# New opening, turned h outside the ring, and two ring slots filled earlier, in a one-core transformer layer kernel

## The chip, the cores and the metric

The kernel runs on one core of one Trainium2 chip. The metric is the device time of one execution in microseconds (us); lower is better. The kernel before takes 429.64 us, the median of three runs (429.25 to 429.87).

## What is computed

One layer for T = 256 tokens of width D = 1024, all in fp32:

```
xn   = rms_norm(h, norm1_g);  proj = xn @ w_in
y    = sigmoid gates * (nsa attention, pooled mixer, short convolution), each projected to D
h    = h + merged @ w_o
h    = h + hier_moe(rms_norm(h, norm2_g), router_group_w, router_expert_w, w1, w3, w2)
out  = rms_norm(h, final_norm_g)
```

`hier_moe` picks one of 4 groups per token and the best 2 of its 8 experts; `out += combine * ((silu(x@w1) * (x@w3)) @ w2)` over 32 experts with a hidden width of 256. The expert weights are 96 MB, read once.

## The kernel before

**Memory.** A ring of 22 slots of 1 MB in SBUF (128 partitions x 2048 floats) first holds the weights of the front half and many work tiles, then the expert weights. The 96 expert chunks (12 for each block of four experts: eight of w1 and w3, four of w2) go through these 22 slots. Slot 20 (SLOT_O) holds `oT`, the attention output, and later `g2b`, the second norm's weights. Slot 21 (SLOT_XHI) holds `xhi`, then `mhi`, then `h2T`, which is h turned for the router. SP issues all large transfers in one fixed order written out by hand (L453 to L564): the two tiles of x, the identity, the front chunks (each two halves, alternating over two sets of slots, a new half waiting for the last product that reads the old one), expert chunks into slots as they come free (`early`, L479), then the other 74 expert chunks, each behind a wait on `expert_used`, the count of chunks that TensorE is done with (L546 to L558).

**Opening (L644 to L662, L847 to L861, L1240 to L1292).** ACT sums the squares of both tiles of x, POOL takes the power -0.5 for both at once, DVE lays the result on two diagonals, and TensorE multiplies h by them (L1244, fp32), which turns and scales in one. ACT rounds a weight half to fp32r (`have_high`, L434), DVE takes the rest (`have_low`, L441); the same is done to the turned x (L660, L858). A product is three fp32r matmuls. The products for q need all of the first half of the q weights split before the first of them. The order is a outside, k inside.

**Middle.** Projections, attention, mixers and merge gates fill TensorE up to W_o (L1517 to L1519). For W_o there are two chunks, each of two halves.

**From W_o to the experts (L1095 to L1176, L1540 to L1610).** DVE adds W_o's result to h in four pieces, ACT sums their squares (L789), TensorE turns h with 16 transposes (L1543), ACT and DVE copy the result to `h2T`. The router product (L1552) has h2T stationary and 40 columns of router weights moving, 16 matmuls. DVE scales and biases the logits (L1116) and picks groups and experts in a row of small steps up to `mask_done`; meanwhile TensorE does six matmuls without use (`keep_busy(6)`, L1558). POOL multiplies tile 1 of h by g2b (L613), DVE makes tile 0 of xn2 (L1110), ACT scales tile 1 (L798). Slot 21 is filled when the logits are done, slot 20 when xn2 is done. TensorE then gathers the tokens of the first four experts (L1589; k = 0 to 5 ahead of the loop, 6 and 7 in it), ACT copies the first half of the gather (L812, first instruction in its loop), and the expert products begin (L1619).

**Expert loop.** Eight blocks. Each has the first products over eight chunks, silu, a transpose, four second products (L1646), each with a copy on ACT (L819), a combining product (L1656) and adds on DVE (L1202). In the fourth and eighth block, two idle matmuls follow each of the chunks q = 4 to 7.

**End (L821 to L831, L1223 to L1232, L628 to L635, L559 to L563).** ACT sums squares of h in three column ranges; POOL adds epsilon, multiplies half of tile 1 by the final weights and adds a partial sum; DVE multiplies the other half; POOL takes the power; ACT scales tile 1, DVE tile 0; SP issues four output transfers.

```
for c in range(SLOTS, NC):
    sp.wait_ge(expert_used, earlier(c) + 1)
    sp.dma_start(ring[:, AT[c]], experts[c // NQ, c % NQ]).then_inc(expert_in[AT[c]], 16)
```

## Time and profile before

| | |
|---|---|
| median of the runs | 429.64 us |
| the profiled execution's own time | 429.46 us |
| its span | 427.7 us |
| PE busy | 395.8 us (93%) |
| DVE, ACT, POOL busy | 202.1, 152.7, 14.7 us |
| DMA over the span | 140.18 MB, mean 328 GB/s |

The span runs from the first to the last instruction in the profile; 1.76 us of the execution's own time lie around it. In the page of the profile, the span is cut into 40 slices of 10.7 us. The rate of the DMA stands between 419 and 423 GB/s in nearly all slices from the 22nd to 38th, and is uneven before. PE is at 90% or more of nearly every slice up to the 20th, which says only that some matmul was in flight.

### The profile page before, as it was taken

The numbers are of one execution on the slowest core, as the hardware profiler recorded it, in microseconds if no ns is written. First come the engines' busy times: TensorE is split into PE (matmuls) and PEld (weight loads), VectorE is DVE, ScalarE is ACT, GpSimd is POOL, SyncE is SP. The second block draws the span as 40 slices with busy tenths as digits, with TensorE's granted clock in tenths as the row PEclk, the third lists the DMA queues.
The fourth block names the chain that finished last, engine by engine and source line by source line (L and its number), as shares of the span: only waits on it lengthen the run. The fifth ranks groups of instructions, "written<-read, shape, count | busy, mean of one in ns | idle before, by whom it ended". The sixth has DMA issues, their size and how long they took to land.

```text
span 427.7 us, 7303 instructions
## 1 busy us (share of the span) xinstructions
PE 395.8 (93%) x2858; PEld 269.9 (63%) x2858; DVE 202.1 (47%) x404; ACT 152.7 (36%) x260; POOL 14.7 (3%) x35
## 2 busy tenths in 40 slices
PE   1999999999999999999999999999999889698892
PEld 1999899767777777878784646454646245143361
DVE  0937493999898685683471232231131303114014
ACT  4823531738565635342312223230132213013014
POOL 2000000300000000000220000000000000000002
PEclk9999999999999999999989999999999969889897
DMA  8988999742442594557997999999999999999972
GB/s 302 399 326 335 364 387 382 296 147 98 149 156 62 185 359 161 208 198 308 424 410 313 421 419 420 421 421 418 421 421 423 421 421 422 421 421 422 421 306 98
DMA packets 21192, 140.18 MB, mean 328 GB/s; under 512 B 2608, under 2 KB 3120, under 8 KB 5040
## 3 DMA queue, kind: packets, MB, share of 16 engines
q1 hardware_dynamic: 20160, 138.32, 81.4%
q10 hardware_dynamic: 1008, 1.52, 1.0%
q8 instruction: 17, 0.28, 0.3%
q14 instruction: 7, 0.06, 0.0%
HBM read 138.78 MB, written 1.05 MB: 327 GB/s over the span
## 4 chain that ended last, share of the span: by engine, by line
issue 46%; PE 45%; DVE 5%; POOL 1%; DMA 1%; ACT 0%; POOLq 0%; ACTq 0%; DVEq 0%; SPq 0%
PE bank L1396 5%; PE bank L1397 4%; PE bank L1398 4%; PE bank L1255 4%; PE bank L1256 4%; PE bank L1257 4%; PE bank L1517 2%; PE bank L1519 2%; PE bank L1518 2%; PE bank L1358 1%; PE bank L1244 1%; PE bank L1384 1%; PE bank L1370 1%; DMA h<-in_x 1%; PE bank L1552 1%
## 5 line engine op out<-in xcount | busy, mean ns | idle before, releaser
L1619 PE MATMUL bank<-ring,kv 128*32 128x512 f32 x512 | 67.0, 641 | 12.5 <-DMA ring<-in_experts 11.9
L441 DVE TENSOR_TENSOR part<-ring,part 128x2048 fp32r<-128x2048 f32 (+1 forms) x28 | 61.9, 2219 | 21.7 <-ACT part L434 21.7
L434 ACT CAST part<-ring 128x2048 fp32r<-128x2048 f32 (+1 forms) x28 | 51.8, 1850 | 35.8 <-DMA ring<-in_front 35.7
L1202 DVE TENSOR_TENSOR h<-h,bank 128x256 f32<-128x256 f32 x64 | 27.0, 421 | 67.2 <-PE bank L1656 66.8
L1589 PEld LDWEIGHTS bank<-qcur,att 128*128 128x128 f32 x280 | 34.8, 195 | 17.4 <-issue 17.2
L1619 PEld LDWEIGHTS bank<-ring,kv 128*32 128x32 f32 x512 | 13.7, 112 | 48.0 <-issue 25.3
L1589 PE MATMUL bank<-qcur,att 128*128 128x128 f32 x280 | 39.9, 288 | 0.6 <-DVE qcur L1165 0.6
L1396 PE MATMUL bank<-part,xhi 128*128 128x512 f32 x96 | 39.3, 409 | 0.0
L1397 PE MATMUL bank<-part,xhi 128*128 128x512 f32 x96 | 37.6, 391 | 0.0
L1398 PE MATMUL bank<-part,xlo 128*128 128x512 f32 x96 | 37.6, 391 | 0.0
L1656 PE MATMUL bank<-gab,vbd 128*128 128x256 f32 x128 | 36.2, 405 | 0.7
L1255 PE MATMUL bank<-xhi,part 128*128 128x256 f32 x128 | 36.7, 287 | 0.0
L1256 PE MATMUL bank<-xlo,part 128*128 128x256 f32 x128 | 36.2, 283 | 0.0
L1257 PE MATMUL bank<-xhi,part 128*128 128x256 f32 x128 | 36.2, 283 | 0.0
L1646 PE MATMUL bank<-ring,hidT 128*32 128x256 f32 x512 | 34.3, 385 | 0.1
L814 ACT ACTIVATE cw<-bank 128x256 f32<-128x256 f32 x8 | 3.1, 383 | 85.0 <-PE bank L1619 85.0
L1656 PEld LDWEIGHTS bank<-gab,vbd 128*128 128x128 f32 x128 | 21.0, 188 | 16.1 <-DVE h L1202 10.5
L819 ACT COPY gab<-bank 128x256 f32<-128x256 f32 x32 | 11.9, 372 | 53.9 <-PE bank L1646 53.9
L1196 DVE TENSOR_TENSOR vbd<-cw,bank 128x256 f32<-128x256 f32 x8 | 3.4, 421 | 56.5 <-ACT cw L814 56.5
L1255 PEld LDWEIGHTS bank<-xhi,part 128*128 128x128 f32 x128 | 24.5, 191 | 0.8 <-issue 0.8
L1256 PEld LDWEIGHTS bank<-xlo,part 128*128 128x128 f32 x128 | 24.5, 192 | 0.0
L1257 PEld LDWEIGHTS bank<-xhi,part 128*128 128x128 f32 x128 | 24.5, 192 | 0.0
(229 smaller groups left out, 551.2 us busy)
## 6 DMA issues: line engine op xcount, KB each, us to landing
ring<-in_experts SPq DMA_DIRECT2D x96, 1024.0 KB, 17.9
ring<-in_front SPq DMA_DIRECT2D x30, 1024.0 KB, 5.4
ring<-in_projs SPq DMA_DIRECT2D x4, 512.0 KB, 4.7
ring<-in_front SPq DMA_DIRECT2D x2, 560.0 KB, 6.4
h<-in_x SPq DMA_DIRECT2D x2, 512.0 KB, 3.9
out_y<-att SPq DMA_DIRECT2D x4, 256.0 KB, 2.4
con<-in_consts SPq DMA_DIRECT2D x1, 764.0 KB, 11.0
oT<-in_vecs ACTq DMA_DIRECT2D x1, 512.0 KB, 6.4
```

Source lines behind the costliest of these rows:

```text
L434: nc.scalar.copy(high(n, half)[:, 0:c].bitcast(F32R), raw(n, half)[:, 0:c]).then_inc(hi_done, 1)
L441: nc.vector.tensor_tensor(low(n, half)[:, 0:c].bitcast(F32R), raw(n, half)[:, 0:c], high(n, half)[:, 0:c], ALU.subtract).then_inc(split_do ...
L1255: mm(dst, whi, ahi, start=start, stop=False)
L1256: mm(dst, whi, alo, start=False, stop=False)
L1257: return mm(dst, wlo, ahi, start=False, stop=stop)
L1396: mm(bank[t][:], XH[:, kk, cols], whi[:, k], start=(kk == 0), stop=False)
L1397: mm(bank[t][:], XH[:, kk, cols], wlo[:, k], start=False, stop=False)
L1398: ins = mm(bank[t][:], XL[:, kk, cols], whi[:, k], start=False, stop=(kk == KT - 1))
L1589: ins = mm(bank[2 + k // 4][:, (k % 4) * P:(k % 4 + 1) * P], xn2[:, t, k * P:(k + 1) * P], flat(sel[:, t]), start=(t == 0), stop=(t == NT ...
L1619: ins = mm(bank[0][CAP * e:CAP * (e + 1)], xgT[:, q, CAP * e:CAP * (e + 1)], expert(j, q, e), start=(q == 0), stop=(q == NQ1 - 1))
L1646: ins = mm(second_out(qt, slice(CAP * e, CAP * (e + 1))), hT[:, ht, CAP * e:CAP * (e + 1)], second_weights(j, qt, ht, e), start=(ht == 0), ...
L1656: mm(combined(t), cmbT[:, t * P:(t + 1) * P], yN[:, qt * QC:(qt + 1) * QC], start=True, stop=True).then_inc(comb_done, 1)
```

## The change

Six parts, by their place in the program:

1. Opening: the q weights' first transfers are cut in two (`first_in`); x is scaled by DVE (`scale_x`, four pieces of 512 columns), with the power taken per tile; TensorE turns it with transposes instead of products with a diagonal; four idle matmuls stand ahead; splits and products of q go by pairs of k, k outside and a inside; four small transfers of ACT's queue are issued later.
2. `h2T` moves from slot 21 to `kv` and `gab`; `g2b` moves from slot 20 to `con`. Slot 20 is filled after `oT_done`, between the two chunks of W_o in SP's order; slot 21 directly behind slots 16 to 18, at W_o's end.
3. Router: the router weights, padded to 64 columns, are stationary and h2T moves, even k in the first and odd k in the last 64 output rows; ACT copies the result, two matmuls with `fold2` add the halves and turn them back. POOL multiplies all four pieces of h by g2b, ACT scales both tiles.
4. Gather: k = 0 to 3 ahead of the loop, 4 to 7 in two pieces in it; ACT's first copy stands ahead of its loop.
5. The idle matmuls behind chunk q = 7 go.
6. End: ACT's first squares stand ahead of the last block's last copy; POOL multiplies three quarters of tile 1 early, DVE one quarter; the partial sums are one DVE instruction; the last output transfer is issued by ACT.

```diff
-            front_chunk(CH_Q, 0)
-            front_chunk(CH_Q, 1)
+            for half in range(2):
+                for sem_in, c in ((first_in[half], slice(0, 1024)), (chunk_in[slot(CH_Q, half)], slice(1024, 2048))):
+                    sp.dma_start(raw(CH_Q, half)[:, c], front[CH_Q, half, :, c]).then_inc(sem_in, 16)
...
-            for i in range(2):
-                front_chunk(CH_WO + i, 0)
-                front_chunk(CH_WO + i, 1)
+            front_chunk(CH_WO, 0)
+            front_chunk(CH_WO, 1)
+            sp.wait_ge(oT_done, 2)
+            early(SLOT_O, SLOT_XHI)
+            front_chunk(CH_WO + 1, 0)
+            front_chunk(CH_WO + 1, 1)
...
             early(SET_B + 2, SLOT_MERGED)
-            sp.wait_ge(logit_full, 1)
             early(SLOT_XHI, SLOTS)
-            sp.wait_ge(xn2_done, NT)
-            early(SLOT_O, SLOT_XHI)
...
+            for t in range(NT):
+                pool.wait_ge(ssq_done, t + 1)
+                step(nc.gpsimd.tensor_scalar(stat[:, 20 + t:21 + t], stat[:, t:t + 1], EPS, None, ALU.add))
+                nc.gpsimd.tensor_tensor(stat[:, 22 + t:23 + t], stat[:, 20 + t:21 + t], stat[:, 32:33], ALU.pow).then_inc(rstd_done, 1)
...
+            q_high(0, 0)
+            q_high(0, 1)
+            act.wait_ge(prm_in, 16)
+            x_high(0)
...
+            gathered_copy(0)
             act.wait_ge(passes_done, 1)
...
+            scale_x(0, 0)
+            scale_x(0, 1)
+            q_low(0, 0)
+            scale_x(1, 0)
+            scale_x(1, 1)
+            x_low(0)
+            x_low(1)
+            q_low(0, 1)
...
+            pe.wait_ge(zeros_set, 9)
+            keep_busy(4, pcw[:, 0, 0:P], pcw[:, 0, 0:2 * P])
+            for t in range(NT):
+                for k in range(KT):
+                    if k % 4 == 0:
+                        pe.wait_ge(scaled, 2 * t + k // 4 + 1)
+                    ins = nc.tensor.transpose(xT(k)[:, t * P:(t + 1) * P], xs[:, t, k * P:(k + 1) * P], ident)
...
-                for t in range(NT):
-                    ins = mm(bank[(0, 3)[t]][:, 0:RC], h2T[:, k, t * P:(t + 1) * P], rw[:, k], start=(k == 0), stop=(k == KT - 1))
+                ins = mm(bank[0][HD * (k % 2):HD * (k % 2) + HD, 0:T], rw[:, k], h2T[k], start=(k < 2), stop=(k >= KT - 2))
+            ins.then_inc(lgT_full, 1)
+
+            pe.wait_ge(lgT_done, 1)
+            for t in range(NT):
+                ins = mm(bank[3][:, t * RC:(t + 1) * RC], lgT[:, t * P:(t + 1) * P], fold2, start=True, stop=True)
...
-            gather(0, 1, 2, 3, 4, 5)
+            gather(0, 1, 2, 3)
...
-                        if q == 2:
-                            gather(6, 7)
+                        if q in (1, 2):
+                            gather(2 * q + 2, 2 * q + 3)
...
-                        if j == ROUND - 1 and q >= 4:
+                        if j == ROUND - 1 and 4 <= q < NQ1 - 1:
...
-                    gather(3, 4, 5)
+                    gather(3)
...
-            nc.vector.tensor_tensor(fin[:, 1, HALF:D], h[:, 1, HALF:D], fing[:, HALF:D], ALU.mult).then_inc(gained, 1)
+            nc.vector.tensor_tensor(fin[:, 1, 3 * QC:D], h[:, 1, 3 * QC:D], fing[:, 3 * QC:D], ALU.mult).then_inc(gained, 1)
+            dve.wait_ge(ssq_done, 3 * NT + 2 * NT)
+            nc.vector.scalar_tensor_tensor(stat[:, 28:30], stat[:, 12:14], EPS, stat[:, 14:16], ALU.add, ALU.add).then_inc(means_done, 1)
...
+            act.wait_ge(act_fin, 2)
+            act.dma_start(out[P:2 * P, HALF:D], fin[:, 1, HALF:D]).then_inc(out_done, 16)
```

## Rows read from the trace of the kernel before

**Rows 1.** Stages: window, its length, busy time (instructions) of each engine, clock, DMA share, GB/s.

```profile
226.80:229.60 2.80, 2.70 (x23) 1.28 (x24) 0.00 (x0) 1.13 (x1) 0.00 (x0) 1.00 0.33 56
229.60:414.40 184.80, 172.17 (x1409) 85.45 (x1412) 42.99 (x115) 39.26 (x67) 0.00 (x0) 0.95 1.01 420
```

**Rows 2.** Timeline of SP's queue around the start of the experts: start, length, what.

```profile
217.14 0.81 SPq L482 DMA_DIRECT2D ring<-in_experts  x2
...
228.02 1.19 SPq L548 DMA_DIRECT2D ring<-in_experts  x2
```

**Rows 3.** Timeline of TensorE in the last expert block (idle time and releaser in brackets).

```profile
398.24 1.94 PE L1619 MATMUL bank<-ring,kv 128*32 128x512 f32 x8 [1.42 <-DMA ring<-in_experts]
...
405.92 1.07 PE L1619 MATMUL bank<-ring,kv 128*32 128x512 f32 x8
...
416.27 1.07 PE L1646 MATMUL bank<-ring,hidT 128*32 128x256 f32 x16
```

**Rows 4.** Timeline of the opening, all engines, and SP's issue at the first q end.

```profile
4.12 1.06 ACT L649 ACTIVATE squares<-h 128x1024 f32<-128x1024 f32 x1 [1.32 <-DMA h<-in_x]
...
5.65 1.06 ACT L649 ACTIVATE squares<-h 128x1024 f32<-128x1024 f32 x1 [0.38 <-DMA h<-in_x]
...
7.28 0.71 POOL L588 TENSOR_TENSOR stat<-stat 128x2 f32<-128x2 f32 x1
...
8.56 5.61 PE L1244 MATMUL bank<-gab,h 128*128 128x128 f32 x32 [8.56 <-DVE gab L850]
9.17 1.90 ACT L434 CAST part<-ring 128x2048 fp32r<-128x2048 f32 x1 [2.37 <-DMA ring<-in_front]
11.10 2.29 DVE L441 TENSOR_TENSOR part<-ring,part 128x2048 fp32r<-128x2048 f32 x1 [2.52 <-ACT part L434]
13.31 3.22 DVE L858 SCALAR_TENSOR_TENSOR xlo<-bank,prm,xhi 128x256 fp32r<-128x256 f32 x8
...
20.11 0.33 SPq L471 DMA_DIRECT2D ring<-in_front  x1
```

**Rows 5.** Timeline of ACT and DVE at the third half of W_o's weights.

```profile
186.59 1.92 ACT L434 CAST part<-ring 128x2048 fp32r<-128x2048 f32 x1 [0.72 <-DMA ring<-in_front]
...
190.49 2.28 DVE L441 TENSOR_TENSOR part<-ring,part 128x2048 fp32r<-128x2048 f32 x1
```

**Rows 6.** Timeline from W_o's end to the first expert product; the sixth row is a window.

```profile
209.17 1.30 POOL L613 TENSOR_TENSOR att<-h,oT 128x512 f32<-128x512 f32 x1 [123.52 <-DVE h L1099]
...
213.37 3.74 PE L1552 MATMUL bank<-rw,h2T 128*128 128x40 f32 x32 [0.48 <-ACT h2T L794]
...
216.94 4.52 PE L1558 MATMUL bank<-con 128*128 128x256 f32 x12
217.15 0.43 DVE L1116 SCALAR_TENSOR_TENSOR qT<-bank,stat,rb 128x40 f32<-128x40 f32 x2 [1.26 <-PE bank L1552]
...
223.19 2.92 PE L1589 MATMUL bank<-qcur,att 128*128 128x128 f32 x24 [0.56 <-DVE qcur L1165]
...
218.00:220.00 2.00, 2.00 (x6) 1.55 (x6) 1.76 (x8) 0.22 (x1) 0.00 (x0) 0.50 0.99 401
...
224.75 1.28 ACT L812 ACT_TABLE_LOAD   x1 [3.71 <-DVE npass L1160]
...
226.90 1.93 PE L1619 MATMUL bank<-ring,kv 128*32 128x512 f32 x16 [0.57 <-ACT kv L812]
```

**Rows 7.** Chain that ended last, in order of time: products on four column strips.

```profile
43.53 1.86 PE bank L1316 x32
```

**Rows 8.** Timeline of the end: DVE, POOL, ACT and SP.

```profile
420.11 1.14 DVE L1225 TENSOR_TENSOR att<-h,con 128x512 f32<-128x512 f32 x1
...
420.65 0.65 POOL L633 TENSOR_TENSOR stat<-stat 128x2 f32<-128x2 f32 x1
...
422.38 1.33 ACT L831 ACTIVATE att<-att,stat 128x512 f32<-128x512 f32 x2 [1.77 <-POOL stat L635]
...
423.17 1.81 SPq L563 DMA_DIRECT2D out_y<-att  x4
```

More of the change, by code:

```diff
@@ L266, in build @@
         vec_in = sem("vec_in")
+        first_in = [sem(f"first_in{half}") for half in range(2)]
         chunk_in = {s: sem(f"chunk_in{s}") for s in (0, 1, 2, 3, *range(SET_A, SET_B + 4, 2))}
@@ L417, in before, with splits, q_pair @@
             return [m for m in range(n) if slot(m, 0) == slot(n, 0)]
+        def splits(n, half):
+            return 4 * (half + 1) if n == CH_Q else 8 + 2 * (SPLITS.index(n) - 1) + half + 1
+        def q_pair(half, pair):
+            return [w[:, 512 * pair:512 * (pair + 1)] for w in (raw(CH_Q, half), high(CH_Q, half), low(CH_Q, half))]
         def floats(n):
@@ L650, in _, with q_high, x_high @@
                                      scale=D ** -0.5, accum_out=stat[:, t:t + 1]).then_inc(ssq_done, 1)
+            def q_high(half, pair):
+                if pair < 2:
+                    act.wait_ge(first_in[half], 16)
+                else:
+                    landed(act, CH_Q, half)
+                r, hi, lo = q_pair(half, pair)
+                nc.scalar.copy(hi.bitcast(F32R), r).then_inc(hi_done, 1)
+            def x_high(k):
+                act.wait_ge(xT_full, k + 1 if k < 6 else KT)
+                nc.scalar.activation(xhi[:, k].bitcast(F32R), xT(k), ACT.Copy,
+                                     scale=prm[:, PR_G1 + k:PR_G1 + k + 1]).then_inc(xhi_done, 1)
+            q_high(0, 0)
+            q_high(0, 1)
+            act.wait_ge(prm_in, 16)
+            x_high(0)
+            x_high(1)
+            x_high(2)
+            q_high(0, 2)
+            x_high(3)
+            x_high(4)
+            q_high(0, 3)
+            x_high(5)
+            x_high(6)
+            x_high(7)
+            for pair in range(4):
+                q_high(1, pair)
+            have_high(act, CH_KV, 0)
             act.dma_start(flat(cw2[:]), small).then_inc(small_in, 16)
@@ L805, in _, with gathered_copy, hidden @@
             nc.scalar.activation(e2, behind, ACT.Exp).then_inc(exp_done, 1)
+            def gathered_copy(b):
+                act.wait_ge(xg_full, b * 2 + 2)
+                nc.scalar.copy(flat(xgT[:, 0:4]), bank[2][:]).then_inc(xg0_done, 1)
+            def hidden(after):
+                act.wait_ge(hid1_full, after)
+                nc.scalar.activation(sl1, bank[0][:, 0:HID], ACT.Silu).then_inc(silu_done, 1)
+                act.wait_ge(hT_full, after)
+                nc.scalar.copy(flat(hT), bank[1][:, 0:HT * P]).then_inc(hT_done, 1)
@@ L1263, in split @@
             def split(n, half):
-                pe.wait_ge(split_done, 2 * SPLITS.index(n) + half + 1)
+                pe.wait_ge(split_done, splits(n, half))
             XH, XL = xhi[:].bitcast(F32R), xlo[:].bitcast(F32R)
@@ L1280, in pair @@
                 ins.then_inc(full, 1)
-            split(CH_Q, 0)
-            w = parts(CH_Q, 0, 2 * P)
-            for a in range(2):
+            for half in range(2):
+                w = parts(CH_Q, half, 2 * P)
                 for k in range(KT):
-                    if a == 0:
+                    if half == 0:
                         pe.wait_ge(xnT_done, k + 1)
-                    ins = product(bank[4][:, a * T:(a + 1) * T], w[0][:, k, a * P:(a + 1) * P], w[1][:, k, a * P:(a + 1) * P],
-                                  XH[:, k], XL[:, k], k == 0, k == KT - 1)
-            ins.then_inc(q_full, 1)
-            pair(bank[5], CH_Q, 1, q_full)
+                    if k % 2 == 0:
+                        pe.wait_ge(split_done, 4 * half + k // 2 + 1)
+                    for a in range(2):
+                        ins = product(bank[4 + half][:, a * T:(a + 1) * T], w[0][:, k, a * P:(a + 1) * P], w[1][:, k, a * P:(a + 1) * P],
+                                      XH[:, k], XL[:, k], k == 0 and a == 0, k == KT - 1 and a == 1)
+                ins.then_inc(q_full, 1)
             pair(bank[0], CH_KV, 0, kvc_full)
```

198 lines of the change are left out of this document (111 added, 87 removed).

## The prediction

> **What bounds the kernel now.** I first cut the span at the places where the DMA's rate changes (busy time by windows). From 229.6 to 414.4 us the DMA is full: share 1.01, 420 GB/s [rows 1]. These 184.8 us carry the 74 expert chunks that do not fit in the 22 slots at first, so 184.8 / 74 = 2.50 us a chunk. In the 2.8 us before, the share is 0.33: the ring is full and nothing may be sent. SP's queue shows the ends of this gap: the last two slots are asked for at 217.14, the next chunk only at 228.02, when TensorE is done with the first one [rows 2]. TensorE's first expert product starts at 226.90 [rows 6].
>
> The reader is to see three stages. Up to 226.9 TensorE and what feeds it set the pace. From there 74 x 2.50 us follow, whatever TensorE does. Then comes a tail: in the last block TensorE waits 1.42 us for chunk q = 4 at 398.24; counting on in steps of 2.50, q = 7 arrives at 405.7 and the last of w2 at 415.7; TensorE takes q = 7 at 405.92 and the last at 416.27 [rows 3], 0.2 and 0.6 us behind.
>
> So the time is (start of the experts) + (stream) + (tail). A slot that is filled earlier shortens the stream only if the ring would not be full otherwise. It is full 2.8 us before the stream starts again.
>
> **The slots, part 2.** Two transfers of 2.50 us leave the stretch behind W_o: one goes ahead of it, one moves from the logits to W_o's end. The ring is then full about 2.5 us earlier (224.3 by the old clock, since only one transfer leaves the full stretch). Alone I book 0. It is cover for the other parts: they can pull the first freed slot from 228.0 toward 224.3 before filling would bind, 3.7 us against the 2.2 found below. The transfer into slot 20 now stands ahead of W_o's second chunk on SP's queue, its wait on `oT_done` before the waits of W_o's second chunk. 2.5 us there delay W_o's third half by 0.6 at most, since SP asks for that half only when a later product ends. ACT takes this half at 186.59 after 0.72 us of waiting, but DVE only at 190.49, 2.0 us after ACT is done [rows 5]. Cost 0; bound 0 to 0.6.
>
> **The opening, part 1.** Before: the second sum of squares runs 5.65 to 6.8, the power ends at 7.99, TensorE turns x from 8.56 for 5.6 us, and the first product waits for that and for DVE [rows 4]. The first q half ends at 20.11, where SP's next request is released; TensorE's pairs are 5.76 us apart from there. After, from the same rows:
> - Tile 0: squares end 5.3, power 1.2 later, 6.5; DVE scales two pieces. A 512-column piece costs 0.45 to 0.69 (2.29 us for 2048 columns with two inputs, a quarter is 0.6 to 0.7). Done near 7.4.
> - q weights: the full half lands at 9.17 [rows 4]; its first part, if sent first, 1.3 us before, near 7.9. ACT rounds it (a third of 1.90, 0.6), DVE splits it to 9.15, scales tile 1 to 10.1.
> - Turning follows the scaling. At 0.23 a matmul, as in the gather (2.76 / 12 [rows 6]), the last is done by 11.0; ACT, in its order, wants it only at 13.2.
> - ACT then makes eight x pieces and two quarters by 14.4, DVE eight pieces of 0.40 (3.22 / 8) and three quarters of 0.7 by 15.8 [rows 4]. The last k can start at 15.8, its six matmuls take 0.7: 16.5 to 17.2.
> - 20.1 minus 17.2 gives 2.9. The second half needs DVE's quarters at 16.5 to 18.5, TensorE wants them from 17.2 in steps of 1.4: covered.
> I take 2.6, for a part of the landing that isn't split so cleanly. Bounds: 3.2 (landing not last) and -1.5, below. The later small transfers are needed at the pooled mixer near 71 us: 0. Later front chunks are requested by TensorE's own progress, so they move along; the 2.6 reach W_o's end whole.
>
> One resource is shared here. DVE's last product takes 1.14 us while POOL is in a 1.30 us product; other tensor products of 512 columns take 0.69 [rows 8]. In the opening POOL's steps for tile 1 meet DVE's scaling of tile 0, at most 0.45 us, and tile 1 waits for the split of q until 9.15 anyway: 0 in my sum. The Trainium skill (SBUF — State Buffer, "Who interferes with whom") says that DVE and GpSimd share a port pair as an exclusive lock. By that rule POOL would stand still for two whole pieces of 0.69, tile 1's power would come at 8.0 + 1.4 = 9.4 instead, and the sum below would be 6.05. The trace agrees so far as DVE's product was drawn out beside POOL's; who gives way, it does not show.
>
> **The router, parts 2 and 3.** TensorE's 16 router matmuls run from 213.37 for 3.74 us, and DVE reads the logits at 217.15 [rows 6]. After: eight matmuls of 256 columns. On four column strips, 16 matmuls of 256 columns take 1.86 us [rows 7], 0.12 each; on two strips I take 0.24 each, 1.9 in all (bounds 1.0 and 3.8, without any overlap). ACT's copies come 0.3 earlier by the new order, so 212.95 + 1.9 = 214.9; a 256-column copy 0.4 to 0.5; two fold matmuls 0.5 (0.234 each, from 3.74 / 16). Logits at 216.0: gain 1.15, bounds -0.7 and 2.0. POOL's four products of 1.30 [rows 6] end at 213.1 as its two do now, each following h's pieces 1.35 apart; the power is ready at 214.5, ahead of need. ACT's scalings (2 x 1.15) end near 217.7, and its exponentials are wanted at 220: 0. The six idle matmuls take 4.52 us, partly at clock 0.50 [rows 6], beside DVE's choice of experts, which is as long; all at half clock (12 records of 256 columns, 0.43 each) they take 5.1 and make TensorE late by up to 0.9. I take 0.15 off.
>
> **The gather, part 4.** The 24 records are twelve matmuls and take 2.76 net (2.92 less what the last one overlaps); eight matmuls instead of twelve end 0.9 earlier. But ACT's copy now waits for a table load of 1.28 us from 224.75 [rows 6], which ends at 226.03. Ahead of the loop, a copy behind exponentials needs no load, as in the attention. The copy then starts 0.1 after the gather's end, and the product follows: 225.85 instead of 226.90. Gain 1.05 (bounds 0.4, if TensorE's loop entry is then late, and 1.3). Parts 3 and 4 together: 2.05; one more piece of the gather between the first two chunks delays the second freed slot by 1.1, hidden by 2.50 for the first.
>
> **Parts 5 and 6.** Without the idle matmuls behind q = 7 the last block is 0.7 us faster, and the shorter gather gives 1.1; only 0.6 count, since then the last chunk's arrival binds [rows 3]. The partial sum on POOL (420.65, 0.65) behind its long product, and DVE's 1.14 product, go from the path; DVE's final sum comes at 420.3 less that 0.6 instead of 421.4: 0.6. The four output requests take 1.81 [rows 8], the last now goes out on ACT beside them: 0.45. Sum 1.65, bounds 0.8 and 2.1.
>
> **Sum.** 2.6 + 2.05 + 1.65 = 6.3 us. The profiled execution took 429.46 (span 427.7), 0.18 under the median: 429.46 - 6.3 = 423.2.
>
> **Rivals.**
> - *The opening gives little* (0.17): the two parts of a weight half land together at 9.17, so DVE scales tile 1 1.2 us later, and TensorE is at its slow clock in the products. For it: the 16 turning matmuls took 0.35 each, against 0.23 for such matmuls later [rows 4, 6]. Opening about 0.5: 425.3. The Trainium skill (TensorE: Matmul & The Clock Gate, "Part 1: The HAM clock gate") says that the clock starts at half and activity releases it. By that rule the four idle matmuls at the start speak for the forecast, and the gap behind them for this rival.
> - *The front swallows the shift* (0.10): a weight chunk lands by bytes and not by request, and 2.6 us are lost before W_o: 425.8. Against: ACT and DVE have 2 us of slack at the row I checked [rows 5].
> - *The slots pay for themselves* (0.03): if the stream, not the first freed slot, were the limit, two chunks or 5.0 us more: 418.2. Against: the gap of 2.8 us.
> - *Slower* (0.05): TensorE stays at 1.2 GHz through the gappy opening and again behind the router, which is now short bursts around a copy. At half speed from 10.9 to 21 us the q products end at 27.3 instead of 25.9, a loss of 1.5; idle matmuls overrun by 0.9, and eight gather matmuls cost 1.9 more, with 0.5 for rank and count. 429.46 + 1.5 + 3.3 - 2.05 - 1.65 = 430.6. It decides if the granted clock behind 214 is 0.50 up to the gather; before it was 0.50 from 218 to 220 alone [rows 6].
> - The rest, 0.05, lies near no change.
>
> **Numbers.** The forecast has 0.60. A difference under 0.2%, 0.9 us, can hardly be told from none. Faster 0.88, same 0.05, slower 0.07. The range goes from the best bounds of all three terms, 429.46 - (3.2 + 3.3 + 2.1) = 420.9, to past both weak cases: 420.9 to 426.4.
>
> **What would show it.** SP's second request of the front for the q slot at 17.5 instead of 20.11; the first logits' row on DVE 3.6 to 3.8 earlier; no table load ahead of the first gathered copy; the first freed slot near 223.4, a longer gap in the DMA before it, and then 184.8 us at 420 GB/s again; the last w2 product within 0.1 us of its chunk; three output requests on SP. It would be wrong if the stretch at 420 GB/s got shorter by chunks, or if the first q half ended later than 19.

## The result and the profile after

The changed kernel takes 427.34 us, the median of 12 runs (426.09 to 429.89), against 429.70 us (428.79 to 430.78) for the kernel before beside it. The ratio is 0.9946, 95% interval 0.9925 to 0.9967. It is faster, by 2.3 us; the forecast was 6.3, and 427.34 lies above the range's end of 426.4.

The profiled execution of the changed kernel took 429.35 us. It belongs to an upper group of four of the 12 runs, at 429.15 to 429.89; the other eight lie at 427.5 or below. So the table below also has the profile of a repeat of the same kernel (427.12 us, near the median; 427.66 us as median of 10, ratio 0.996, interval 0.9933 to 0.9987). Each cell is a gain in us over the profile of before, between two marks in the timelines. The spans are 427.7 before, 425.3 and 427.5 after.

| step, from mark to mark | forecast | repeat | profiled |
|---|---|---|---|
| opening: SP's request at the end of the first q half (20.11; 18.85; 19.74) | 2.60 | 1.26 | 0.37 |
| from there to the logits on DVE (217.15; 214.68; 215.65) | 1.15 | 1.21 | 1.13 |
| logits to the first expert product (226.90; 223.32; 225.66) | 0.90 | 1.11 | -0.26 |
| first expert product to the last of w2 (416.27; 414.55; 416.81) | 0.60 | -1.86 | -1.78 |
| last of w2 to POOL's last power (421.64; 419.22; 421.48) | 0.60 | 0.70 | 0.70 |
| power to the end of the span | 0.45 | -0.02 | 0.04 |
| sum | 6.30 | 2.40 | 0.20 |

Three rows fail: the opening, the stream and the output. One depends on the execution: the way from the logits to the experts.

The stream's row holds two gains of opposite sign. Between them lies the moment at which TensorE takes chunk q = 4 of the last block, for which it waits in all three traces (398.24 before [rows 3], 397.12 in the repeat, 399.36 in the profiled execution). From the first expert product to this moment it takes 171.34 us before, 173.80 in the repeat and 173.70 in the profiled execution: 2.4 us lost, where nothing was forecast. From there to the last of w2 it takes 18.03 before and 17.43 and 17.45 now: the forecast 0.6 us, gained.

SP's queue in the profiled execution of the changed kernel, columns as in [rows 2], answers to [rows 2, 4]:

```profile
19.74 0.33 SPq L489 DMA_DIRECT2D ring<-in_front  x1
...
226.78 0.33 SPq L567 DMA_DIRECT2D ring<-in_experts  x1
...
228.87 0.33 SPq L567 DMA_DIRECT2D ring<-in_experts  x1
...
230.96 1.19 SPq L567 DMA_DIRECT2D ring<-in_experts  x2
```

Before, the first two chunks were asked for together, from 228.02, and the third at 230.97. Now the first is 1.24 us earlier, the second is 2.09 behind it, and the third is where it was. The windows of the same kernel show what that does to the stream (columns as in [rows 1]):

```profile
222.00:223.00 1.00, 1.00 (x6) 1.00 (x6) 0.51 (x3) 0.00 (x0) 0.34 (x2) 0.50 1.07 438
...
229.00:230.00 1.00, 1.00 (x12) 0.87 (x15) 0.06 (x1) 0.00 (x0) 0.00 (x0) 1.00 1.07 451
...
232.00:233.00 1.00, 1.00 (x16) 0.39 (x12) 0.00 (x0) 0.00 (x0) 0.00 (x0) 1.00 0.90 336
233.00:234.00 1.00, 1.00 (x16) 0.26 (x8) 0.00 (x0) 0.00 (x0) 0.00 (x0) 1.00 1.20 262
234.00:235.00 1.00, 1.00 (x12) 0.13 (x4) 0.00 (x0) 0.00 (x0) 0.00 (x0) 1.00 0.67 279
```

The DMA reaches its full rate at 229, moves the two chunks that it has been given, and dips to 262 to 336 GB/s from 232 to 235, because the third was asked for only at 230.96. Before, these three windows read 426, 434 and 434 GB/s.

Timeline of the opening after, all engines (answers to [rows 4]):

```profile
6.28 0.88 DVE L940 TENSOR_SCALAR xs<-h,stat 128x512 f32<-128x512 f32 x2 [5.17 <-POOL stat L619]
...
6.92 0.68 POOL L619 TENSOR_TENSOR stat<-stat 128x1 f32<-128x1 f32 x1
8.37 1.14 ACT L679 CAST part<-ring 128x512 fp32r<-128x512 f32 x2 [1.88 <-DMA ring<-in_front]
9.02 0.69 DVE L946 TENSOR_TENSOR part<-ring,part 128x512 fp32r<-128x512 f32 x1 [1.85 <-ACT part L679]
9.63 0.88 DVE L940 TENSOR_SCALAR xs<-h,stat 128x512 f32<-128x512 f32 x2
10.16 1.97 PE L1361 MATMUL bank<-con,xs 128*128 128x128 f32 x8 [2.19 <-DVE xs L940]
...
11.86 0.58 PE L1367 MATMUL bank<-xhi,part 128*128 128x256 f32 x1
```

TensorE turns tile 0 by 8.0, stands idle for 2.19 us until DVE has scaled tile 1, and takes 1.97 us for tile 1's eight transposes, which took 1.06 for tile 0. The granted clock is 0.50 (1.2 GHz) from 10 to 16, and the first products start 0.21 us apart instead of 0.12. In the repeat it was back at 1.00 by 14.

Timeline from W_o's end to the experts after (answers to [rows 6]):

```profile
213.35 1.08 PE L1664 MATMUL bank<-gab,rw 128*64 128x256 f32 x8
214.49 0.37 ACT L854 COPY qcur<-bank 128x256 f32<-128x256 f32 x1 [1.32 <-PE bank L1664]
...
214.91 0.64 PE L1669 MATMUL bank<-con,qcur 128*128 128x40 f32 x4 [0.47 <-ACT qcur L854]
215.38 2.84 PE L1352 MATMUL bank<-con 128*128 128x256 f32 x12
...
219.82 0.43 PE L1675 MATMUL bank<-qT,con 128*128 128x64 f32 x2 [1.61 <-DVE qT L1247]
...
224.84 0.59 ACT L870 COPY kv<-bank 128x512 f32<-128x512 f32 x1 [5.30 <-PE bank L1700]
...
225.66 1.07 PE L1730 MATMUL bank<-ring,kv 128*32 128x512 f32 x8 [0.64 <-ACT kv L870]
225.75 1.28 ACT L875 ACT_TABLE_LOAD   x1 [0.33 <-issue]
```

The router is as forecast, and the copy finds no table load ahead of it. But the six idle matmuls now take 2.84 us, not 4.52, and leave TensorE idle for 1.61 us ahead of the rank product; the granted clock is 0.50 from 221 to 224, and the gather runs at half speed.

The end after (answers to [rows 3, 8]; TensorE at chunk q = 4 of the last block, its last three groups of w2, then POOL, SP and ACT):

```profile
399.36 1.06 PE L1730 MATMUL bank<-ring,kv 128*32 128x512 f32 x8 [1.43 <-DMA ring<-in_experts]
...
411.84 1.07 PE L1757 MATMUL bank<-ring,hidT 128*32 128x256 f32 x16 [0.28 <-DMA ring<-in_experts]
...
414.32 1.07 PE L1757 MATMUL bank<-ring,hidT 128*32 128x256 f32 x16 [0.35 <-DMA ring<-in_experts]
...
416.81 1.07 PE L1757 MATMUL bank<-ring,hidT 128*32 128x256 f32 x16 [0.35 <-DMA ring<-in_experts]
...
421.48 0.71 POOL L655 TENSOR_TENSOR stat<-stat 128x2 f32<-128x2 f32 x1 [1.28 <-DVE stat L1337]
...
423.01 1.33 SPq L581 DMA_DIRECT2D out_y<-att  x3
423.59 0.35 ACTq L920 DMA_DIRECT2D out_y<-att  x1
```

TensorE now waits for each of the last chunks; in this trace the stream binds to the end, as forecast. It only arrives late.

### The profile page after: what moved, and what is told of

Read it like the earlier page. It is cut to its first block, busy times and chain, and to the rows that moved or that the text cites. A ratio compares the mean times of both kernels' runs of the same rounds, so it can differ in the third digit from the quotient of the medians.

```text
span 427.5 us, 7244 instructions
## 1 busy us (share of the span) xinstructions
PE 395.5 (93%) x2820; PEld 265.7 (62%) x2820; DVE 201.7 (47%) x412; ACT 142.3 (33%) x259; POOL 17.9 (4%) x38
## 4 chain that ended last, share of the span: by engine, by line
PE 59%; SPq 19%; DMA 10%; DVE 6%; issue 3%; ACT 1%; POOL 1%; POOLq 0%; DVEq 0%; PEldq 0%
SPq L576 18%; DMA ring<-in_experts 7%; PE bank L1730 7%; PE bank L1509 5%; PE bank L1700 4%; PE bank L1511 4%; PE bank L1510 4%; PE bank L1367 4%; PE bank L1368 4%; PE bank L1369 4%; PE bank L1757 3%; PE bank L1767 3%; DMA ring<-in_front 3%; PE bank L1630 2%; PE bank L1632 2%
## 5 line engine op out<-in xcount | busy, mean ns | idle before, releaser
L455 DVE TENSOR_TENSOR part<-ring,part 128x2048 fp32r<-128x2048 f32 (+1 forms) x26 | 57.4, 2213 | 18.5 <-ACT part L448 18.5
L448 ACT CAST part<-ring 128x2048 fp32r<-128x2048 f32 (+1 forms) x26 | 48.0, 1848 | 33.1 <-DMA ring<-in_front 33.1
L1700 PE MATMUL bank<-qcur,att 128*128 128x128 f32 x272 | 42.6, 298 | 0.5 <-DVE qcur L1272 0.5
L1730 PEld LDWEIGHTS bank<-ring,kv 128*32 128x32 f32 x512 | 12.7, 111 | 45.0 <-DMA ring<-in_experts 22.4
L1367 PE MATMUL bank<-xhi,part 128*128 128x256 f32 x128 | 37.5, 293 | 0.0
L1369 PE MATMUL bank<-xhi,part 128*128 128x256 f32 x128 | 37.0, 289 | 0.0
L1367 PEld LDWEIGHTS bank<-xhi,part 128*128 128x128 f32 x128 | 25.5, 199 | 1.0 <-issue 0.8
L1368 PEld LDWEIGHTS bank<-xlo,part 128*128 128x128 f32 x128 | 25.5, 199 | 0.0
L1369 PEld LDWEIGHTS bank<-xhi,part 128*128 128x128 f32 x128 | 25.4, 198 | 0.0
```

What stands on the lines that cost most here:

```text
L448: nc.scalar.copy(high(n, half)[:, 0:c].bitcast(F32R), raw(n, half)[:, 0:c]).then_inc(hi_done, 1)
L455: nc.vector.tensor_tensor(low(n, half)[:, 0:c].bitcast(F32R), raw(n, half)[:, 0:c], high(n, half)[:, 0:c], ALU.subtract).then_inc(split_do ...
L1367: mm(dst, whi, ahi, start=start, stop=False)
L1368: mm(dst, whi, alo, start=False, stop=False)
L1369: return mm(dst, wlo, ahi, start=False, stop=stop)
L1700: ins = mm(bank[2 + k // 4][:, (k % 4) * P:(k % 4 + 1) * P], xn2[:, t, k * P:(k + 1) * P], flat(sel[:, t]), start=(t == 0), stop=(t == NT ...
```

## The experiments

Every run stands beside runs of the kernel before (medians 429.71 to 429.82). Medians of one kernel are given with the lowest and the highest run.

**1. The same kernel again, and its halves.** `again` is unchanged. `open_only` is the kernel before with part 1 alone; `rest_only` is the changed kernel with the old opening.

> The changed kernel once more, for its spread and a second trace. Its twelve times lie in two groups, 426.1 to 427.5 and 429.1 to 429.9, which the kernel before does not show so clearly. Theory C (clock): TensorE falls to 1.2 GHz in the opening's gap, or ahead of the gather, in some executions and not in others; a trace of a time near 426.5 shows the opening's products at full clock (first q half ends near 17.5 instead of 19.74) or the eight gather matmuls in 1.9 instead of 3.4 us. Rival S (stream): both groups look alike up to the first freed slot, and the 74 chunks take 2 to 3 us more in one of them.

> The kernel before with the new opening alone (part 1). Theory C: the opening gains 0.4 us where the clock falls in the gap before the second tile is turned and up to 2.5 where it does not; the first freed slot, and with it the end, come earlier by the same: 427.3 to 429.3, and not all runs alike. Rival S: the opening's gain does not reach the end at all, since the stream takes up what it gains: 429.6.

> The changed kernel with the opening of before (parts 2 to 6 alone). Theory C: the router gains 1.1 us, the gather loses 1.5 at half clock and gains 1.1 by the table load, so the first slot is freed 0.7 to 1.0 earlier, or 2.3 where the clock holds; the end parts give 0.2 to 1.6: 426.5 to 428.8. Rival S: 429.6 or more, with the stream longer than 185 us.

`again`: 427.66 us (426.65 to 430.31), as given above. `open_only`: 429.18 us (427.49 to 430.37), ratio 0.9976, 0.9953 to 1.0. `rest_only`: 430.05 (427.13 to 431.15), ratio 0.9978, 0.9951 to 1.0005. By the ratios each gives about 1.0 us. By the medians, against 429.74 beside them, it is 0.6 faster and 0.3 slower: nine of the 27 runs of the kernel before lie between 430.76 and 433.57 here, which its median does not show. So neither part alone can be told from no change.

In its trace each shows one of the losses by itself. `open_only`, with the old gather, needs 189.15 us from the first expert product to the last of w2, against 189.37 before. `rest_only` needs 191.5, with a gather of 3.75 us at clock 0.50. So the longer stream is not the opening's, and the opening alone gains 1.53 (18.58 instead of 20.11). The three kernels' executions also spread more than I had reckoned with: `again` runs from 426.65 to 430.31. Between its profile and that of the changed kernel the opening differs by 0.89 us and the gather by 1.38, while the stretch from the first product to the last of w2 is the same (191.23 and 191.15): theory C, not rival S (the stream). In the timeline of `again`:

```profile
214.41 2.84 PE L1352 MATMUL bank<-con 128*128 128x256 f32 x12
...
218.86 0.43 PE L1675 MATMUL bank<-qT,con 128*128 128x64 f32 x2 [1.62 <-DVE qT L1247]
...
220.44 2.02 PE L1700 MATMUL bank<-qcur,att 128*128 128x128 f32 x16 [0.50 <-DVE qcur L1272]
...
222.50 0.59 ACT L870 COPY kv<-bank 128x512 f32<-128x512 f32 x1 [3.92 <-PE bank L1700]
223.32 1.06 PE L1730 MATMUL bank<-ring,kv 128*32 128x512 f32 x8 [0.61 <-ACT kv L870]
```

The same idle time of 1.62 us ahead of the rank product, yet the clock stayed at 1.00, and the gather took 2.02 us instead of 3.40.

**2. The two gaps bridged.** `bridge_open` puts idle matmuls into the gap behind tile 0, `bridge_router` three more behind the router:

```diff
+                if t == 0:
+                    for _ in range(4):
+                        mm(bank[4][:, 0:2 * P], pcw[:, 0, 0:P], pcw[:, 0, 0:2 * P], start=True, stop=True)
```

```diff
-            keep_busy(6, ident, con[:, K_TRI:K_TRI + 2 * P])
+            keep_busy(9, ident, con[:, K_TRI:K_TRI + 2 * P])
```

> The changed kernel with four idle matmuls more, behind the turning of tile 0, in the time in which TensorE waits for tile 1. Theory C: the clock stays at 2.4 GHz, the first q half ends near 17.4 in place of 19.74, and everything up to the first freed slot moves by 2.3 us; median near 425 to 426. Rival S: the opening is faster but the end moves by under 0.5 us against the changed kernel.

> The changed kernel with nine idle matmuls instead of six behind the logits, to fill DVE's choice of experts. Theory C (clock): the six end 1.6 us ahead of the rank product, the clock falls there, and in three of four traces so far the eight gather matmuls run at 1.2 GHz (3.25 to 3.75 us, against 2.02 in the fourth). With nine the gap is about 0.3 us, the gather takes 2.0 in this trace, and the first expert product comes 8.6 to 8.7 us behind the logits instead of 9.9 to 10.4; the runs spread less, median 426.5 to 427.2. Rival: the clock falls anyway, or the nine run past the choice at half clock; then no faster than the changed kernel.

`bridge_open`: 426.92 us (425.35 to 427.99), ratio 0.9923, 0.9898 to 0.9948. The opening keeps clock 1.00 throughout, but its q end is only at 18.68, not 17.4, and the median misses the expected 425 to 426. In this execution the first part of the weights landed at 9.08, and the first product stands at 12.42, 3.34 us behind it; in the six other traces with this order of the opening it stands 3.49 or 3.50 us behind the landing. The gather still ran at half speed (3.25 us). `bridge_router`: 427.29 (426.86 to 427.61, 8 runs), ratio 0.9916, 0.9883 to 0.9948. Its granted clock is 1.00 from 208 to 228, the gather takes 2.02, and none of its runs lies above 427.61, where 4 of the 10 of `again` lay above 429. The median hardly moves, the spread goes: the clock in the gather explains the upper group of the changed kernel's runs (8 of 22 at 429.15 or above, none of 8 here), not the missing 4 us.

**3. The gather cut as before.**

```diff
-            gather(0, 1, 2, 3)
+            gather(0, 1, 2, 3, 4, 5)
...
-                        if q in (1, 2):
-                            gather(2 * q + 2, 2 * q + 3)
+                        if q == 2:
+                            gather(6, 7)
...
-                    gather(3)
+                    gather(3, 4, 5)
```

> The changed kernel with the gather cut as before (k = 0 to 5 ahead of the first expert product, 6 and 7 behind chunk 1), ACT's copy still ahead of its loop. Theory R (second freed slot): with a piece of the gather behind chunk 0, the second slot is freed 2.1 us after the first instead of 1.0, and the stream from the first expert product to the last w2 product is 190.8 to 191.5 us in four traces, against 189.1 and 189.4 with the old cut. Here it should be 189.0 to 189.6, with the first product 0.3 to 0.6 later behind the logits: the end 1.3 to 1.6 us earlier. Rival: the stream's length varies with the chip's memory and has nothing to do with the cut; then 190.5 to 191.5 again.

425.97 us (425.18 to 426.64), ratio 0.9896, 0.9861 to 0.9931: undoing this one piece of part 4 takes 1.4 us off the changed kernel's median, and it is 1.3 below `bridge_router`, which was run beside it. SP's queue, and two windows of the stretch where the changed kernel dips:

```profile
225.08 1.19 SPq L567 DMA_DIRECT2D ring<-in_experts  x2
...
228.02 1.19 SPq L567 DMA_DIRECT2D ring<-in_experts  x2
```

```profile
231.00:232.00 1.00, 1.00 (x12) 0.13 (x4) 0.00 (x0) 0.00 (x0) 0.00 (x0) 1.00 1.07 451
232.00:233.00 1.00, 1.00 (x11) 0.82 (x8) 0.26 (x1) 0.39 (x1) 0.00 (x0) 1.00 0.98 418
```

The first two requests stand together again, and there is no dip. TensorE at chunk q = 4 of the last block, in the same timeline:

```profile
396.09 1.60 PE L1730 MATMUL bank<-ring,kv 128*32 128x512 f32 x8 [1.43 <-DMA ring<-in_experts]
```

This gives the stream in two pieces, in us:

| | first product to third request | third request to q = 4 of the last block |
|---|---|---|
| before | 4.07 | 167.27 |
| changed kernel, profiled | 5.30 | 168.40 |
| `again` | 5.30 | 168.50 |
| `gather_old` | 4.06 | 168.07 |

The first column is the cut's, 1.2 us. The second is 168.09 to 168.70 in the six traces with the new cut and 167.98 to 168.07 in `gather_old`, `gather_bridge` and `best`, so up to 0.7 us go with the dip (0.3 and 0.4 in this table). The other 0.8 us stay with the old cut. In the ten traces of kernels with parts 3 to 6 the DMA's mean rate from 236 to 395 is 419 or 420 GB/s, in the four without them 421; over these 159 us that is 0.4 to 0.8 us. No run shows where it comes from.

From the first expert product to the last of w2 it is 189.57 us. With the new cut it was 191.15, 191.23, 191.5, 190.83, 190.9 and 191.4 in six traces; with the old cut it was between 189.1 and 189.6 in five of eight traces of this study, and in the other three (190.87 in `slots_only`, 190.69 in `best`, 192.36 in `best_slots_late`) TensorE ran two products of the last block at half speed, as shown below; in `best_slots_late` the slots come in too. Nor does the old cut start much later: from the logits to the first product it takes 8.82 us, against 8.64 in `again`. The product waits for ACT's copy of k = 0 to 3, which starts 2.06 us into the gather in both; k = 4 and 5 run beside that copy.

**4. Another order in the opening.** ACT makes the first pieces of x, and DVE scales tile 1, ahead of the q weights; three idle matmuls behind the turning.

```diff
-            q_low(0, 0)
             scale_x(1, 0)
             scale_x(1, 1)
...
             x_low(0)
+            q_low(0, 0)
```

> The changed kernel with another order in the opening: DVE scales tile 1 before it splits the first pair of q, ACT's and DVE's x pieces go ahead of the q pairs, and three idle matmuls follow the turning. Theory L (landing): the first part of the q weights lands no earlier than 8.4 to 9.1 us, nearly as late as the whole half did (9.17), and DVE's queue held tile 1 behind it. With tile 1 free of it, the first product starts near 10.8 instead of 11.9 to 12.4 and the first q half ends near 16.7 at full clock (18.68 in the best trace so far). The end 1.5 to 2.0 us ahead of the changed kernel's good runs. Rival: the q half still ends past 18, since something else holds it.

427.53 us (424.53 to 429.42), ratio 0.9923, 0.989 to 0.9955. The q end is at 18.16, not 16.7: the 16 transposes took 3.67 us, at half speed, and behind them the idle matmuls, 1.68 us from 10.70, stood in front of the first product at 12.03. The rival fits: the median is that of the changed kernel. The gather ran at half speed here too (3.46 us), so the median does not tell what the order alone is worth.

**5. The slots alone**, in the kernel before, with six idle matmuls and then with nine (`slots_bridge`, the same edit of `keep_busy` as above). Both also have the change's order of ACT's squares and copies of the turned h.

> The kernel before with the slots alone: turned h in kv and gab, g2b in con, slot 20 filled between W_o's two chunks, slot 21 at W_o's end. Theory: the ring is full 2.5 us earlier and waits longer; the first freed slot and the end stay: 0 to 0.5 us (ACT's copies for the router come 0.3 earlier). Rival (the slots pay for themselves): 2.5 to 5 us faster.

> The kernel before with the slots of the change alone (turned h and the second norm's weights outside the ring, the two fills at and ahead of W_o's end) and nine idle products in place of six. It tells whether the slots alone, which came out at 430.9 with the gather's 24 matmuls at half clock (5.46 us), cost anything of their own. Theory (they are worth nothing, and the loss was the clock in the gather): gather 2.92 us at clock 1.00, first expert product at 226.6 to 227.0, 189.2 to 189.8 us from there to the last chunk's second product, 429.0 to 429.9. Rival (the DMA traffic of the two fills beside W_o and the router slows W_o's end or the gather's neighbours): gather at full clock and logits still 0.3 us or more behind 217.15, 430.3 to 431.0. Rival (they help once the clock is mended): under 190 from first product with the last at 415.8 or earlier, 428.0 to 428.9.

With six: 430.92 us (429.06 to 433.42), ratio 1.002, 0.9991 to 1.0049. With nine: 429.84 (428.81 to 430.21), ratio 0.9989, 0.9974 to 1.0004. The profile with six shows what the moved slots do not cause themselves:

```profile
217.23 2.84 PE L1572 MATMUL bank<-con 128*128 128x256 f32 x12
221.61 0.41 PE L1577 MATMUL bank<-qT,con 128*128 128x32 f32 x2 [1.55 <-DVE qT L1154]
...
223.48 5.46 PE L1603 MATMUL bank<-qcur,att 128*128 128x128 f32 x24 [0.42 <-DVE qcur L1179]
```

In the profile with nine the gather takes 2.92 us, as before, and the first product comes at 226.50. So the slots are worth 0 within 1 us here, and the clock in the gather is a trap of the old code too. Of the 12 runs with six idle matmuls, six lie at 431.18 or above; of the 12 with nine, none above 430.21. The traces of all kernels say the same: where six idle matmuls end 1.55 to 1.62 us ahead of the rank product, the clock was at 0.50 in all or most of the gather in five of seven; with nine (0.26 to 0.33 us), at 1.00 in all five. The kernel before has such an upper group as well (19 of 66 runs beside these experiments above 430.7); no trace of such a run was taken, so its cause is not shown.

**6. The best version found.** `gather_bridge` is the changed kernel with the old cut and nine idle matmuls. `best` is that with the other order of the opening, without idle matmuls behind the turning. `best_slots_late` is `best` with the two slots filled where the kernel before fills them.

```diff
-            sp.wait_ge(oT_done, 2)
-            early(SLOT_O, SLOT_XHI)
...
+            sp.wait_ge(logit_full, 1)
             early(SLOT_XHI, SLOTS)
+            sp.wait_ge(xn2_done, NT)
+            early(SLOT_O, SLOT_XHI)
```

> The changed kernel with two edits together: the gather cut as in the kernel before (pieces 0 to 5 ahead of the first expert product, 6 and 7 behind chunk 1, twelve instructions of two matmuls' width as there), and nine idle products in place of six ahead of the rank product. Theory (two separate costs, the cut of the gather and a granted clock that falls in the gap behind the idle products): the gather lies at clock 1.00 in every execution, 2.9 us for 24 matmuls; logits at about 215, first expert product at 223.9 to 224.1, and 189.1 to 189.6 us from there to the last chunk's second product, as with the old cut; so 425.4 to 426.4 as median, with a spread under 1.5 us between fastest and slowest. Rival (the old cut alone already keeps TensorE busy enough, so the three idle products more add nothing and only lie ahead of the rank product): 425.9 to 426.6, same as the old cut alone to 0.2. Rival (the gain of the old cut was luck of the executions): 427.0 to 427.5, and over 190.5 us from first expert product to the last.

> As the run with the old cut and nine idle products, and the opening in another order: tile 1 is scaled ahead of the splitting of q's first half, x's pieces are made ahead of it too, and no idle matmuls are put behind tile 0's turning. Theory (the opening's end is set by when q's weights have landed and are split, and by TensorE's own 5.8 us from its first product): SP's request at the end of the first q half at 18.0 to 18.6, logits at 214.2 to 214.8, 424.9 to 425.7 as median. Rival (the splitting on VectorE is now late, so the new order loses what it wins): request at 18.9 to 19.7 and 425.8 to 426.5. Rival (the front's gain is swallowed ahead of the experts): logits at 215 or later with the request at 18.3.

> As the run before it on this chip (old cut, nine idle products, reordered opening), but the two freed ring slots are filled where the kernel before fills them: one behind the logits, the other behind the second norm, and not at and ahead of W_o's end. Theory (the ring is full anyway by the time the first expert product frees a slot, so the early slots are worth nothing): same to 0.3 us, first freed slot's request at 224.6 to 225.2 with the queue idle before it. Rival (with the experts starting 2 us earlier than before the fill of the ring ends as late as the first slot comes free, about 225, so each microsecond of an early slot counts): the request for the first freed slot still lands behind a fill in progress, last second product 0.5 to 2.4 us later, 425.9 to 427.5.

| | median (lowest to highest) | ratio, interval |
|---|---|---|
| `gather_bridge` | 426.17 (425.27 to 426.42) | 0.9907, 0.9885 to 0.993 |
| `best` | 424.45 (423.12 to 426.11) | 0.9861, 0.9835 to 0.9887 |
| `best_slots_late` | 424.96 (423.17 to 426.49) | 0.9867, 0.9841 to 0.9894 |

`gather_bridge` does not tell its first two theories apart: 426.17 fits both, so nine idle matmuls added nothing that shows here. Luck is ruled out (189.57 us again). `best` beats both kernels: it is 5.4 us below the median of before and about 3 below the changed kernel, and lies below the 424.9 to 425.7 that its theory gave. It differs from `gather_bridge` in the opening alone, and is 1.7 faster: there q ended at 18.44 (in the fastest of its six executions), here at 17.80 (in an execution of 426.11 us, the slowest of its six), and at 16.59 in `best_slots_late`, which has the same opening (in an execution of 426.49, also the slowest of its six). The two timelines (`best` first) differ in one thing:

```profile
7.56 3.67 PE L1361 MATMUL bank<-con,xs 128*128 128x128 f32 x16 [1.46 <-DMA con<-in_consts]
11.69 0.45 PE L1367 MATMUL bank<-xhi,part 128*128 128x256 f32 x1 [0.46 <-DVE part L946]
```

```profile
7.42 1.97 PE L1362 MATMUL bank<-con,xs 128*128 128x128 f32 x16 [1.59 <-DMA con<-in_consts]
10.57 0.36 PE L1368 MATMUL bank<-xhi,part 128*128 128x256 f32 x1 [1.19 <-DVE part L947]
```

The same 16 transposes take 3.67 or 1.97 us. All that follows is shifted by this: the first product by 1.12, the q end by 1.21.

For the slots, the medians (0.5 apart, each with a spread of 3) decide nothing. The profile of `best_slots_late` shows that the cover is used up, though:

```profile
222.00:223.00 1.00, 1.00 (x16) 0.26 (x8) 0.00 (x0) 0.77 (x1) 0.00 (x0) 1.00 0.97 410
223.00:224.00 1.00, 1.00 (x13) 0.58 (x6) 0.00 (x0) 0.00 (x0) 0.00 (x0) 1.00 1.11 270
224.00:225.00 1.00, 1.00 (x14) 0.58 (x16) 0.38 (x1) 0.00 (x0) 0.00 (x0) 1.00 0.64 180
```

The first freed slot's request, at 222.70, finds the fill still going, and the DMA never falls to zero as it does in `best` (0 GB/s from 223 to 224). It starts the experts 1.30 us earlier than `best`, and yet takes its chunks later. TensorE waits for the same chunk, q = 4 of the last block, in both (`best` first):

```profile
394.91 1.93 PE L1730 MATMUL bank<-ring,kv 128*32 128x512 f32 x8 [1.43 <-DMA ring<-in_experts]
```

```profile
395.28 1.94 PE L1731 MATMUL bank<-ring,kv 128*32 128x512 f32 x8 [1.43 <-DMA ring<-in_experts]
```

That is 0.37 us later, and it is 0.37 already at 335.16 and 335.53. So between the first product and there the kernel with the late slots loses 1.67 us in the arrival of its chunks, in one trace of each. This is what the rival said: with the experts this early, an early slot counts. The last w2 product is 0.37 us later, not the 0.5 to 2.4 that it gave. How much of it reaches the runs' times stays open.

From there on both traces go alike, 18.65 us to the last of w2, and TensorE itself is late. In the timeline of `best`:

```profile
398.78 1.94 PE L1730 MATMUL bank<-ring,kv 128*32 128x512 f32 x8
401.86 1.06 PE L1730 MATMUL bank<-ring,kv 128*32 128x512 f32 x8
...
413.56 1.07 PE L1757 MATMUL bank<-ring,hidT 128*32 128x256 f32 x16
```

From 396 to 401 the granted clock is 0.50, and two products take 1.93 and 1.94 instead of 1.06, as one does in [rows 3]; the chunks after them show no wait for the DMA. From here on TensorE sets the end. In `gather_bridge`, whose clock was back at 1.00 by 399, the same stretch takes 17.44, 1.2 less. That is the next thing to mend, and it was not tried.

## Why the prediction was wrong, point by point

**The stream: "74 x 2.50 us follow, whatever TensorE does."** This step failed, and it is the largest term: 2.4 us lost up to chunk q = 4 of the last block, where nothing was to be lost. The start of the stream is not the first freed slot. A restart takes time (228.02 asked, 418 GB/s from 230 in the trace of before), and one chunk covers 2.50 us, so the second and third requests must come in time too. I did price the moved piece: "delays the second freed slot by 1.1, hidden by 2.50 for the first". The delay was right (the two requests stood 0.86 apart before, now 2.09). What I left out is that the third slot needs the same work of TensorE under either cut (24 + 8 gather records, or 16 + 8 + 8), and that TensorE stands idle ahead of the first product with the new one: 0.61 us, waiting for ACT's copy, beside which k = 4 and 5 ran with the old one. From the logits to the third request it takes 13.82 us before, 13.94 in `again`, 13.93 in `bridge_router` and 12.88 in `gather_old`, all with the gather at clock 1.00; so parts 3 and 4 together gained 0.9 us at this request with the old cut and nothing with the new one. In the profiled execution, with the gather at half speed, this request moved by 0.01 us, whatever the first one gained. The third request is the mark to count from. Of the 2.4 us, 1.2 lie ahead of this request, 0.3 to 0.4 go with the dip behind it, and 0.8 stay with the old cut, unexplained. The Trainium skill (DMA: Bandwidth & Descriptors, "Anatomy of one DMA — SWDGE (gpsimd) path") puts a fixed part of about 2.0 us on one transfer on that path. The 2 us from the request to full rate in the trace are of that size, but they are another quantity, and the queue here is SP's.

**The gather, part 4: mechanism right, its cut worth nothing.** The table load did leave the path. At clock 1.00 the gain from the logits to the first product is 1.11 (0.9 forecast), but it comes from the copy (3.71 us from the gather's start to the product before, 3.07 with the old cut, 2.88 with the new), and 0.29 from the shorter choice of experts (6.04 to 5.75). The four gather matmuls taken out gave 0.19, not 0.9, since k = 4 and 5 can run beside the copy, as they do with the old cut; at the third request they cost 1.06.

**The opening: 2.6 forecast, 0.4 to 1.5 measured.** Two errors. The first part of the weights lands at 8.23 to 9.08 over the traces, not 7.9, nearly as late as the whole half before (9.17); the whole half landed at 8.94 to 9.32 over the four traces that ask for it in one. And I built the end from DVE's last piece ("the last k can start at 15.8"), where TensorE's own products need 6.0 to 6.3 us from the first one at clock 1.00, up to 7.9 when part of them runs at 0.50. The first product stood at 11.7 to 12.4 in the seven traces of this order; the one with clock 1.00 throughout ended q at 18.68, the others at 18.44 to 19.74. The prediction named an end of q later than 19 as a sign that it was wrong; it came in the profiled execution, not in the repeat. The rival "the opening gives little" named the late landing and the clock, and gave 0.5.

**The clock.** The rival "slower" put its decision at the granted clock behind 214 up to the gather. In the profiled execution it was 1.00 from 214 to 220 and 0.50 in the gather (3.40 us), and the loss was 1.4 us there, not the 1.9 plus 0.9 that I priced. I had the cause the wrong way round: the idle matmuls do not overrun at half clock, they end early at full clock and leave a gap, and nine of them in place of six take the upper group of runs away. The Trainium skill (TensorE: Matmul & The Clock Gate, "Part 1: The HAM clock gate") says that the same kernel runs a different number of matmuls at half clock at its start from one execution to the next. The traces agree, and show the same later in a kernel: 3.40 and 2.02 us for one gather in two executions of one kernel, 3.67 and 1.97 for the same transposes in two kernels with the same opening.

**The router: right.** 1.21 and 1.13 against 1.15. The eight matmuls on two strips run from 212.44 to 214.43, 1.99 us against the 1.9 taken.

**The front swallows nothing: right.** The logits stand earlier by the opening's gain and the router's: from the q end to them it takes 195.91 and 195.83 us, against 197.04 before.

**The slots: right at 0** in the kernel before (0.9989, 0.9974 to 1.0004), and right as cover: `best_slots_late` reaches the end of it, and its stream is 1.67 us longer. (The cover was compared with 2.2 us; the sum has 2.05.)

**The port between DVE and POOL.** The Trainium skill (SBUF — State Buffer, "Who interferes with whom") calls the port pair that the two share an exclusive lock; by that rule, as the prediction worked it out, tile 1's power was to come at 9.4. It ended at 7.60, beside DVE's scaling from 6.28 to 7.16, and took 0.68 against tile 0's 0.57. The measurement decides: no delay of that length here. It does not refute the rule itself: DVE's pieces took 0.44 us each, not 0.69, and only 0.24 us of the power lay beside them.

**The end.** The power's chain gave 0.70 (0.6 forecast). The output request on ACT gave 0 of 0.45: the last request goes out at 423.59, 0.58 after SP's first, but from the power to the end it is 6.02 us, as it was 6.06 before. I had the issue on the path, and it is not there. The forecast 0.6 us of the last block came, and lies in the stream's row. Its reason holds only where the stream is late: with the new cut TensorE waits for the last chunks, while in `gather_old` and `gather_bridge` it waits for none of the last three.

Left open: why the clock falls in one execution and not in another with the same gap; where the 0.8 us of the stream go that the old cut does not give back; and whether six idle matmuls would do with the old cut (none of the six runs of `gather_old` lies high, and its one trace has the gap and clock 1.00).

## What to carry to other kernels

When a stream restarts from a full ring, count from the second and third freed slot as well as from the first: work moved from ahead of a loop into its first two steps is no gain if the third slot's release needs the same work. An idle matmul that covers a gap is sized by the clock it meets; after a neighbour gets faster, read the gap again and compare the spread of the runs, not their median alone. Before halving a transfer to get its first part early, do not count on half the time: here the first part landed at 8.23 to 9.08, the whole at 8.94 to 9.32.

## What the runs showed of the hardware that I had not expected

- Two idle times of the same length (1.61 and 1.62 us) in two executions of one kernel: clock 0.50 behind one, 1.00 behind the other.
- The clock's column reads 1.00 in the opening of `best` from 2 to 10 us, though its 16 transposes took 3.67 us there, and 1.97 in another execution. The eight records of idle matmuls ahead of them took 3.78 us, 0.47 each, where twelve of the same size took 2.84 at 215.38 in the changed kernel, 0.24 each. In these first microseconds the column and the instructions' own times do not agree; I go by the latter.
- A dip in the stream need not lie where its cause is. The DMA falls to 262 GB/s at 233 (to 172 in `bridge_open`, 180 in `again`, each for 1 us), 4 us behind the late second request in the profiled execution; TensorE waits for none of it there: its first wait for a chunk comes only at 339.60, when it has used up the lead of the ring.
